# A tanh in the swish gate in place of exponential and reciprocal, and a copy out of PSUM moved from VectorE to ScalarE

## The reference

```python
h = rms_norm(x, norm_mix[l])
proj = h @ w_in[l]                  # split into q_a k_a v_a u_b q_c k_c v_c g_c
y_a = sliding_window_sink_attention(q_a, k_a, v_a, ...)
y_b = multiscale_pool(u_b, ...)
y_c = retention(q_c, k_c, v_c, g_c, pos)
x = x + concat(y_a, y_b, y_c) @ w_out[l]
x = x + moe_ffn(rms_norm(x, norm_ffn[l]), ...)   # 32 experts, 2 for each token
```

## Time and profile before

| | |
|---|---|
| runs shown | 3117.36 us median of 3 (3113.74 to 3118.77) |
| the profiled execution's own time | 3114.68 us |
| its span, first to last instruction | 3112.9 us |
| mean granted TensorE clock | 0.997 |
| mixing stage of layer 1, about | 0 to 820 us |
| mixing stage of layer 2, about | 1560 to 2370 us |

### The profile page before, as it was taken

How to read it: one execution, slowest core, us unless ns; L and a number is a source line. 1 busy time by engine, 2 the same in 40 slices (tenths; PEclk the granted TensorE clock), 3 DMA queues, 4 the chain that set the end, 5 groups by cost and what they waited for, 6 DMA issues and landing times.

```text
span 3112.9 us, 55907 instructions
## 1 busy us (share of the span) xinstructions
PE 3051.7 (98%) x18148; PEld 2173.5 (70%) x18148; DVE 1563.0 (50%) x4610; ACT 603.2 (19%) x1890; POOL 1043.8 (34%) x1250
## 2 busy tenths in 40 slices
PE   8999999999899999999999999999998999999998
PEld 4455545554699999888755455455547999998886
DVE  5688888877422222211156888888773222222111
ACT  1222222222211111101113223222221111111101
POOL 1132132233255555423212232221332555564322
PEclk9999999999999999999999999999999999999999
DMA  8756656552689999999865556566527899999996
GB/s 305 264 179 245 214 195 251 211 189 105 257 284 308 318 323 344 342 356 348 323 246 193 188 219 250 179 231 238 182 101 268 288 308 313 324 348 345 345 356 215
DMA packets 248192, 817.18 MB, mean 263 GB/s; under 512 B 68016, under 2 KB 121264, under 8 KB 188720
## 3 DMA queue, kind: packets, MB, share of 16 engines
q1 hardware_dynamic: 201200, 735.20, 63.7%
q0 software_dynamic: 46112, 77.70, 10.7%
q10 hardware_dynamic: 576, 0.52, 0.1%
HBM read 718.87 MB, written 95.56 MB: 262 GB/s over the span
## 4 chain that ended last, share of the span: by engine, by line
PE 73%; DVE 15%; DVEq 5%; issue 4%; DMA 2%; SPq 0%; POOL 0%; ACT 0%; ACTq 0%; POOLq 0%
PE bank L2036 31%; PE bank L1739 10%; PE bank L2076 9%; PE bank L1804 7%; PE bank L2066 6%; PE bank L1710 5%; PE bank L1664 1%; DVE newton L1148 1%; DVE newton L1150 1%; DVE newton L1152 1%; DVE arena L1364 1%; DVE arena L1177 1%; PE bank L1929 1%; PE bank L1890 1%; DMA arena<-in_x 1%
## 5 line engine op out<-in xcount | busy, mean ns | idle before, releaser
L2036 PEld LDWEIGHTS bank<-arena,wts 128*128 128x128 f32 x8192 | 985.4, 191 | 22.1 <-issue 22.1
L2036 PE MATMUL bank<-arena,wts 128*128 128x128 f32 (+7 forms) x8192 | 989.5, 283 | 7.8 <-DVE arena L1618 7.0
L1739 PE MATMUL bank<-wts 128*128 128x512 f32 x1056 | 473.5, 598 | 6.2 <-DVE arena L1280 2.0
L1641 DVE TENSOR_TENSOR arena<-arena,bank 128x128 f32<-128x128 f32 (+6 forms) x64 | 19.2, 300 | 901.6 <-ACT arena L1109 901.6
L1804 PE MATMUL bank<-wts,arena 128*128 128x512 f32 x1024 | 456.1, 598 | 1.6 <-ACT arena L1047 1.6
L1739 PEld LDWEIGHTS bank<-wts 128*128 128x128 f32 x1056 | 193.9, 190 | 231.7 <-issue 215.5
L826 POOL DMA_INDIRECT arena<-hrows,arena x288 | 292.7, 1016 | 167.8 <-issue 151.9
L1804 PEld LDWEIGHTS bank<-wts,arena 128*128 128x128 f32 x1024 | 189.2, 190 | 215.4 <-issue 212.8
L722 POOL TENSOR_TENSOR arena<-arena 128x256 f32<-128x256 f32 x32 | 23.1, 722 | 829.8 <-DVEq L1394 829.8
L851 POOL DMA_INDIRECT out<-arena x176 | 275.1, 1563 | 54.7 <-issue 51.5
L2076 PE MATMUL bank<-arena,wts 128*128 128x135 f32 (+6 forms) x2176 | 280.0, 289 | 0.0
(11 more groups left out here) (264 smaller groups left out, 3246.7 us busy)
## 6 DMA issues: line engine op xcount, KB each, us to landing
wts<-in_w_gate SPq DMA_DIRECT2D x128, 1024.0 KB, 8.3
wts<-in_w_up SPq DMA_DIRECT2D x128, 1024.0 KB, 10.7
wts<-in_w_down SPq DMA_DIRECT2D x128, 1024.0 KB, 17.2
wts<-wt SPq DMA_DIRECT2D x96, 1024.0 KB, 6.7
wts<-in_w_in SPq DMA_DIRECT2D x88, 1024.0 KB, 8.9
hrows<-arena SPq DMA_DIRECT2D x36, 512.0 KB, 7.5
out<-arena SPq DMA_DIRECT2D x36, 512.0 KB, 4.0
wt<-arena SPq DMA_DIRECT2D x16, 1024.0 KB, 4.1
```

Of the source, the lines that this page charges most:

```text
L1739: i = mm(bIP[j in (1, 3, 6)][:, :], own[:, d], ring[k % SLOTS][:, d], start=(d == 0 and j in (0, 1, 3)), stop=(d == 3), skip_group_check=True)
L2036: return mm(gu_at(f, k, w), lhs, xT[:, d, 0:w], start=start, stop=(d == DC - 1), skip_group_check=True)
```

## The change

The gate uses silu(g) = g * (1 + tanh(g/2)) / 2. ScalarE computes tanh(g/2) where it computed exp(-g). VectorE then does one `scalar_tensor_tensor`, (t + 1) * g, in place of three operations. This leaves twice the gate, and the factor 0.5 is the scale of the copy of the turned `yc` on ScalarE. The copy of the turned rotary columns to `rT` goes from the head of VectorE's step to ScalarE, between `kTr` and the tanh. TensorE gets a wait for `hT_ready` ahead of the key-value products.

```diff
@@ ScalarE
                         a(kTr[:, :, :, o], bD[:, 0:256].rearrange("p (g c n) -> p g c n", g=2, c=2), ACT.Copy,
                           scale=kg).then_inc(qkT_ready, 1)
+                        a(rT.rearrange("p j n -> p (j n)"), bE[:, :], ACT.Copy).then_inc(rT_ready, 1)
                         wait_columns(e.wait_ge, l, s - 1, 3)
-                        a(eg, rows_of(s - 1)[:, RG0:RG0 + RW], ACT.Exp, scale=-1.0).then_inc(exp_gate, 1)
+                        a(eg, rows_of(s - 1)[:, RG0:RG0 + RW], ACT.Tanh, scale=0.5).then_inc(tanh_gate, 1)
...
-                        a(mixT[:, 6:8].rearrange("p j n -> p (j n)"), bE[:, 0:256], ACT.Copy).then_inc(ycT_ready, 1)
+                        a(mixT[:, 6:8].rearrange("p j n -> p (j n)"), bE[:, 0:256], ACT.Copy, scale=0.5).then_inc(ycT_ready, 1)
@@ VectorE
-                    if back:
-                        e.wait_ge(pe_qkrT, t0)
-                        v.tensor_copy(rT.rearrange("p j n -> p (j n)"), bE[:, :]).then_inc(rT_ready, 1)
...
-                        e.wait_ge(exp_gate, t0)
-                        v.tensor_scalar(eg, eg, 1.0, None, ALU.add)
-                        e.drain()
-                        v.reciprocal(eg, eg)
-                        e.drain()
-                        v.tensor_tensor(sg, eg, rows_of(s - 1)[:, RG0:RG0 + RW], ALU.mult).then_inc(silu_ready, 1)
+                        e.wait_ge(tanh_gate, t0)
+                        v.scalar_tensor_tensor(out=sg, in0=eg, scalar=1.0, in1=rows_of(s - 1)[:, RG0:RG0 + RW],
+                                               op0=ALU.add, op1=ALU.mult).then_inc(silu_ready, 1)
@@ TensorE
                     if back:
                         rv = rows_of(s - 1)[:, RV0:RV0 + RW]
+                        if s + 2 < TILES:
+                            e.wait_ge(hT_ready, t0 + 3)
```

More of the change, by code:

```diff
@@ L315, in program @@
         pe_ykv, kvd_read, ysq_ready, z_ready = sem("pe_ykv"), sem("kvd_read"), sem("ysq_ready"), sem("z_ready")
-        exp_gate, silu_ready, yc_ready = sem("exp_gate"), sem("silu_ready"), sem("yc_ready")
+        tanh_gate, silu_ready, yc_ready = sem("tanh_gate"), sem("silu_ready"), sem("yc_ready")
         pe_pT, pT_ready, maps_ready, pe_fold, fold_ready = sem("pe_pT"), sem("pT_ready"), sem("maps_ready"), sem("pe_fold"), sem("fold_ready")
```

## The result

The changed kernel takes 3101.85 us (median of 6 runs, 3098.20 to 3104.09), the kernel before 3116.31 us (6 runs, 3113.74 to 3118.77): a ratio of 0.995 with a 95% interval of 0.994 to 0.996, 14.5 us less. The forecast was 3101. The profiled execution took 3100.88 with a span of 3099.0, 13.9 less than the span before.

What follows compares the result with a forecast made beforehand. VectorE was taken to decide in stretches of the mixing stages where TensorE is also nearly full. Gains of 9.5, 6.4 and 0.8 us sum to 16.7, off 3117.4: forecast 3101 us, its own range 3096 to 3106, wider range 3095 to 3112.

Steps and rivals of the forecast that it cites:

- VectorE decides in stretches where TensorE is 98% busy: Mixing stages: both engines are nearly full in stretches and VectorE sets the time; faster engines could win 11.7 us in 22 steps.
- Steps 2 to 13 gain 9.5: Both layers, 22 steps: even steps come down to the length of odd ones, 11.7 less 2.2, so 9.5 us.
- The residue over 46.52: Steps 2 to 13: 0.1 us left in each of 22 steps above the shortest step, 2.2 us off the gain.
- 1.1 us of the gate's saving turn into a wait for `exp_done`: Behind the gate: of 2.15 us saved a step, about 1.0 arrives, since line 1369 then waits for ScalarE's exponentials.
- Steps 14 and 15 gain 1.6 each, 6.4 together: From `add_x` to `z_ready` TensorE waits for VectorE, so line 1369's 1.6 us arrive in full in four steps.
- Step 16 gains 0.8 in both layers: TensorE's wait of 0.38 us for line 1381, behind the gate, goes in each of two layers: 0.8 us.
- The copy costs ScalarE nothing: The moved copy, 0.60 us on ScalarE, lies in idle time ahead of line 923, which waits for TensorE.
- No table load: ScalarE in mixing steps: exp and tanh lie in one table set, so the run keeps its four loads.
- The rivals with loads: ScalarE loads tables twice a step: exp's load delays `exp_done` by 1.28 us, 3112 (0.06), or by 2.57, 3131 (0.05).
- the prediction's rival with a load for exp: Two loads a step; tanh's falls in idle time, exp's delays `exp_done` by 1.28 us: 3112 us, chance 0.06.
- Busy time: Whole run: VectorE's busy time falls by 87 us to 1476, ScalarE's rises by 19 to 622.
- The first rival: Relief only in part: behind line 1380 VectorE's small operations run 0.4 us longer beside GpSimd, 22 steps, 3109.5 us; chance 0.14.

Runs made afterwards that it cites:

- the run with Silu: The changed kernel, but ScalarE computes silu directly and VectorE does nothing for the gate: 3106.67 us, 0.9962 of the kernel before.
- the repetition: The changed kernel measured again with no edit: 3099.98 us, 0.9949 of the kernel before.
- the reordered run: The changed kernel, but in steps 14 and 15 VectorE does query/key norm Newton steps behind the gate and scaling behind `z_ready`: 3094.24 us, 0.9926 of before.

## Why the prediction was right

The forecast was 3101, the result 3101.85. Its steps, one by one:

- *VectorE decides in stretches where TensorE is 98% busy.* Shown by the same work costing 3 to 5 us by the medians (nothing in steps 2 to 13) ahead of line 1375 and over 20 us behind it.
- *Steps 2 to 13 gain 9.5.* They gained 9.0. Even steps came down from up to 47.8 to between 46.5 and 46.9, apart from waits for weights. The residue over 46.52, without these waits, was 0.16 a step on the mean where 0.1 was chosen, 1.3 us in all; 0.8 less of waits for weights gave most of it back. The residue was chosen from a wrong reading: odd steps took not up to 0.1 but up to 0.23 more than 46.52 before (46.75 in step 9), and with the change they take up to 0.34 more.
- *1.1 us of the gate's saving turn into a wait for `exp_done`.* It is 1.10 in step 8 and 1.19 on the mean of 32 steps. Two useless products fit into it unnoticed. Without this step the sum would have had 2.15 in place of 1.0 in steps 14 and 15, 4.6 us too much.
- *Steps 14 and 15 gain 1.6 each, 6.4 together.* From step 13 to 16 it was 6.1, in part by luck. Against the two steps of before without a clock dip, step 14 gained the 1.6, but step 15 only 1.2, for there VectorE's stall of 0.43 fell on the way: 5.6 in all. The two dips of before, which did not come back, added 0.5.
- *Step 16 gains 0.8 in both layers.* The wait of 0.38 went in both. But from the scores to the first expert product it was 48.01 and 47.92 us and is 47.72 and 47.86, so 0.3 and 0.1, half of the term: a later wait, for line 1470, grew from 0.5 to 0.7.
- *The copy costs ScalarE nothing.* Line 923 starts 0.02 later. But hardly any idle time is left ahead of it.
- *No table load.* Four, as before, so the rule of the Trainium skill ("ScalarE: Activation LUTs", section "Table sets: the hidden batching unit") and the trace agree. The rivals with loads did not happen. The nearest thing to them, the run with Silu, which does switch, took 5 to 7 us more than the change, its load ahead of its activation's wait; the prediction's rival with a load for exp reckoned 11.
- *Busy time.* VectorE 1477.8 (1476 forecast), ScalarE 618.1 (622).
- *The small stall beside GpSimd.* The first rival puts the stall of 0.44 at 455.04 us down to GpSimd. But GpSimd is idle from 454 to 456 us in the trace of before, and idle around the stall at 741.02 shown above, and such stalls recur after a like number of instructions in every trace. So GpSimd does not explain them. That the two do slow each other elsewhere is shown at the end.

The sum was 16.7 and the medians moved by 14.5 here and by 16.8 in the repetition, the profiled executions by 13.8. In the traces the mixing stages give 9.0 + 6.1 + 0.35 in step 16, and 0.7 in steps 0 and 1, for which nothing was forecast: 16.1. The two expert stages were 2.2 us longer in the first trace of the change and take this back. They contain no changed instruction. For the first of them the repetition shows scatter; the second was longer in every trace than in the one trace of before, which stays open. The forecast stood on the median of the runs shown, which was 1.0 above that of the later comparison, and the gain was forecast 2.2 above what the medians gave; the two errors partly cancel, so that 3101 against 3101.85 looks closer than the sum was.

The parts were predicted less well than the whole. The copy alone was to give 7 to 9 and gave 6.0, and the gate alone 10 to 12 and gave 7.6. For the copy the term that failed is that of steps 14 and 15, where the clock fell and where VectorE's stalls lay on the way. For the gate it is that of steps 2 to 13, 3.8 us without the waits for weights where 7 were expected, and a clock dip in step 16.

## What to carry to other kernels

When two engines run neck and neck, look in each stretch for the wait that the late engine already has: work saved ahead of it is worth only what passes the next wait, while work added behind it cost nearly its full time here. Before booking a saving, ask what ends second at the next wait; here ScalarE's exponentials ended 1.06 us before VectorE needed them. What a new wait holds is then free time that other work of the same engine can fill: 4.9 us here from step 13 to 16 in two layers. A gain of half a microsecond a step can also be hidden or feigned by a stall or a clock dip that moved, so look where these lie in both traces before the rest is explained.

## What the runs showed of the hardware

- A table load on ScalarE takes 1.28 us with gaps of 0.01 to 0.03 to its neighbours, and it runs ahead of the semaphore wait of the activation that needs it (0.20 us ahead in step 8 of the Silu run).
- TensorE's granted clock fell to its lower level for a few microseconds after a wait of 1.94 us (mean 0.73 over 4 us), as it had in two of four such steps of the kernel before, after waits of 1.74 (0.65 in one of them). Where the waits were 0.73 and 1.19 it stayed at 1.00 in all four steps. The length of the last wait does not decide it alone: after 1.94 us it also stayed at full speed once, and in step 16 of the reordered run it fell after the same wait of 0.81 that left it at 1.00 in the change.
- VectorE stalls for mostly 0.40 to 0.47 us at a time without waiting for any engine or transfer, mostly after 67 to 75 of its instructions or a multiple of that; the cause was not tested. An edit that adds or takes away instructions moves these stalls: in step 15 of the change one lies ahead of the row maxima (741.02 us), in the kernel before the one of that step lies behind `z_ready` (760.80 us).
- VectorE and GpSimd slow each other in this pair of operations. The two useless products took 0.93 us together ahead of line 1375, where GpSimd was idle, and 1.29 behind `z_ready`, where GpSimd multiplied `sg` by `z` in 0.96 us, an operation of 0.72 in all 32 steps of the kernel before. All engines' timeline of the run with work behind `z_ready`:

```profile
396.18 1.29 DVE L1394 TENSOR_TENSOR arena<-cst 128x256 f32<-128x256 f32 x2 [0.17 <-issue]
396.23 0.96 POOL L723 TENSOR_TENSOR arena<-arena 128x256 f32<-128x256 f32 x1 [26.00 <-DVEq L1390]
```
